# FFN weight split paced ahead of the projection, sixteen-fold heads stored by residue, last addition of the chosen and windowed heads on POOL

## The reference

```python
h = rmsnorm(x, g_mix_pre); z = h @ w_in                     # 1024 -> 33 blocks of 128 columns
o_a = nsa_mixer(...)      # 6 heads: compressed + chosen + window of 512, each times a sigmoid gate, added up
o_b = dilated_mixer(...)  # 12 heads in 3 pairs (window, fold) = (128, 1), (512, 4), (2048, 16)
o_c = banded_attention(...)  # 6 heads, window of 128, with sinks
x = x + rmsnorm(concat(o_a, o_b, o_c) @ w_out, g_mix_post)
x = x + rmsnorm(conv_glu_ffn(rmsnorm(x, g_ffn_pre), w_up, conv_w, conv_b, w_down), g_ffn_post)
```

## Time and profile before

| | us |
|---|---|
| runs (3): median, lowest, highest | 3597.2, 3593.09, 3601.05 |
| the profiled execution's own time | 3595.68 |
| its span, first to last instruction | 3593.9 |
| PE busy | 3413.3 (95%) |
| DVE, ACT, POOL busy | 1412.2, 1164.7, 512.1 |
| mean granted clock of PE | 0.978 of full speed |

### The profile page before, as it was taken

The page is one execution under the profiler, slowest core; times in us unless marked ns, Lnnn a source line. Parts: engine busy times, 40 slices in busy tenths (PEclk is TensorE's granted clock), DMA queues, the critical chain, the costliest instruction groups (busy, mean ns, idle before and its releaser), DMA issues. The chain is left out here.

```text
span 3593.9 us, 45309 instructions
## 1 busy us (share of the span) xinstructions
PE 3413.3 (95%) x16530; PEld 2720.9 (76%) x16530; DVE 1412.2 (39%) x3874; ACT 1164.7 (32%) x1980; POOL 512.1 (14%) x409
## 2 busy tenths in 40 slices
PE   8999999995898999999989969999999999999997
PEld 6788888875787876666657858887888788878886
DVE  5111101104666776666654434412541154115421
ACT  5111111114655765455433323301331133104310
POOL 1454444441000012221010000000000000000000
PEclk9999999997999999999989989999999999999999
DMA  6987765566968732332127665566556655665553
GB/s 200 324 289 258 258 224 176 203 228 178 218 166 200 170 93 59 96 94 55 51 77 234 199 218 193 193 234 233 192 196 234 228 196 197 234 216 206 196 191 117
DMA packets 297668, 676.17 MB, mean 188 GB/s; under 512 B 98704, under 2 KB 154512, under 8 KB 283408
## 3 DMA queue, kind: packets, MB, share of 16 engines
q1 hardware_dynamic: 265616, 517.93, 45.1%
q0 software_dynamic: 31840, 155.40, 12.1%
HBM read 496.06 MB, written 185.57 MB: 190 GB/s over the span
## 5 line engine op out<-in xcount | busy, mean ns | idle before, releaser
L1855 PE MATMUL f_banks<-low,f_w_hi 128*128 128x512 f32 x2816 | 871.3, 390 | 27.1 <-DMA f_w_lo<-f_lo 19.8
L1855 PEld LDWEIGHTS f_banks<-low,f_w_hi 128*128 128x128 f32 x2816 | 529.8, 188 | 140.4 <-issue 25.4
L1855 PE MATMUL f_banks<-low,f_w_lo 128*128 128x512 f32 x1408 | 548.8, 390 | 0.0
L1211 PE MATMUL a_ot_ps<-a_turned_w,a_vs 128*65 128x256 f32 (+3 forms) x1452 | 448.7, 421 | 1.1 <-issue 1.1
L493 PE MATMUL z_banks<-h_hi,z_w_hi 128*128 128x512 f32 x972 | 388.3, 399 | 7.0 <-POOL z_w_lo L305 7.0
L493 PE MATMUL z_banks<-h_lo,z_w_hi 128*128 128x512 f32 x972 | 385.3, 396 | 0.0
L493 PE MATMUL z_banks<-h_hi,z_w_lo 128*128 128x512 f32 x972 | 385.2, 396 | 0.0
L1855 PEld LDWEIGHTS f_banks<-low,f_w_lo 128*128 128x128 f32 x1408 | 265.0, 188 | 54.5
L1282 ACT ACTIVATE w_small<-w_small,a_negm 128x128 f32<-128x128 f32 (+3 forms) x510 | 249.4, 519 | 173.4 <-DVE a_negm L1361 108.3
L1875 PE MATMUL f_banks<-f_w_hi,f_g_hi 128*128 128x512 f32 x704 | 278.4, 396 | 0.0
L1875 PE MATMUL f_banks<-f_w_hi,f_g_lo 128*128 128x512 f32 x704 | 278.4, 396 | 0.0
(11 more groups left out here) (212 smaller groups left out, 5302.3 us busy)
## 6 DMA issues: line engine op xcount, KB each, us to landing
f_w_hi<-f_hi SPq DMA_DIRECT2D x264, 512.0 KB, 3.5
f_w_lo<-f_lo SPq DMA_DIRECT2D x264, 512.0 KB, 4.5
z_xs<-in_w_ffn POOLq DMA_DIRECT2D x33, 1024.0 KB, 8.6
f_hi<-z_v_hi POOLq DMA_DIRECT2D x33, 1024.0 KB, 4.9
f_lo<-z_xs POOLq DMA_DIRECT2D x33, 1024.0 KB, 6.4
low<-z_hi SPq DMA_DIRECT2D x48, 512.0 KB, 7.7
z_hi<-st_hi SPq DMA_DIRECT2D x84, 256.0 KB, 4.5
z_lo<-st_lo SPq DMA_DIRECT2D x84, 256.0 KB, 5.1
```

Source lines behind the costliest of these rows:

```text
L1211: last = pe.matmul(ot_ps[0:out_width(g), at:at + count * P], values, rows, start=(x == 0), stop=(x == len(blocks) - 1), skip_group_check=True)
L1855: last = pe.matmul(banks[:, bank, :], w[:, s % RING, c * P:(c + 1) * P], h[:, c, :], start=(c == 0 and x == 0), stop=(c == DC - 1 and x == 2))
```

## The change

Four edits. (1) POOL's loop in `project` starts at j = 1, does `split_w(j + 2)` first and then one `split_v`, two at j = 4, 8 and 12, so that the 33 pieces end at j = 30. (2) The two 4 MB copies are cut into 16 pairs of 256 KB pieces, one pair after each of the blocks 6 to 21. (3) Blocks 7, 8, 18 and 19 (queries and keys of the four heads with fold 16) are written to the staging by residue: a bank's tokens go to all four slots, so that the stores of such a block wait for all four banks, and its first bank waits for all four stores of the block before; `attend` then reads query and keys of fold 16 as 128 neighbouring elements. (4) The addition to `oh` in w and s units goes to POOL (`add_rows`), whose list in `attend` is now ordered by step together with the mixing; DVE's product into `add` waits for POOL's previous addition.

```diff
+RESIDUE_BLOCKS = (7, 8, 18, 19)
+TWICE = (4, 8, 12)
+MOVES = tuple(range(6, 22))
...
+        def by_residue(bank):
+            return bank.rearrange("p (l m a) -> p m a l", m=4, a=4)
+        def residues(tile, n):
+            return tile[:, :, 0:512].rearrange("p m (a l) -> p m a l", a=4)[:, :, :, n * P // 4:(n + 1) * P // 4]
...
-                    sp.wait_ge(w1_moved, 16)
+                    sp.wait_ge(w1_moved, 16 * len(MOVES))
...
-                    sp.wait_ge(zlo_done, lowered_through(j, n))
+                    sp.wait_ge(zlo_done, lowered_through(j, 3 if j in RESIDUE_BLOCKS else n))
...
+                    elif j in RESIDUE_BLOCKS and n == 0:
+                        for m in range(4):
+                            act.wait_ge(stored[m], stores_through(j - 1))
...
+                    if j in RESIDUE_BLOCKS:
+                        act.activation(residues(st_hi, n), by_residue(bank), ACT.Copy).then_inc(zhi_done, 1)
...
+            def move(i):
+                m, c = divmod(i, len(MOVES) // 2)
+                rows = slice(c * (CMP * HD * 2 // len(MOVES)), (c + 1) * (CMP * HD * 2 // len(MOVES)))
+                pool.dma_start(w1_copy[m, rows], w1[m, rows]).then_inc(w1_moved, 16)
+                rows = slice(i * (D // len(MOVES)), (i + 1) * (D // len(MOVES)))
+                pool.dma_start(wo_copy[rows], w_out[rows]).then_inc(wo_moved, 16)
...
-            pool.dma_start(w1_copy, w1).then_inc(w1_moved, 16)
-            pool.dma_start(wo_copy, w_out).then_inc(wo_moved, 16)
-            for j in range(NZ):
-                if j >= 1 and j + 2 < NZ:
+            v = 0
+            for j in range(1, NZ):
+                if j + 2 < NZ:
                     split_w(j + 2)
-                split_v(j)
+                for _ in range(2 if j in TWICE else 1):
+                    if v < NZ:
+                        split_v(v)
+                        v += 1
+                if j in MOVES:
+                    move(MOVES.index(j))
...
+                    if j in RESIDUE_BLOCKS and n == 0:
+                        for m in range(1, 4):
+                            dve.wait_ge(stored[m], stores_through(j - 1))
...
+                        if j in RESIDUE_BLOCKS:
+                            low, high, bank = residues(st_lo, n), residues(st_hi.bitcast(F32), n), by_residue(bank)
+                        dve.tensor_tensor(low, bank, high, ALU.subtract).then_inc(zlo_done, 1)
...
+            def add_rows(g):
...
+                if g % 4 == 0:
+                    pool.wait_ge(oh_in[s], 16 * (m // 2) + 16)
+                pool.wait_ge(added, g - late + 1)
...
+                pool.tensor_tensor(rows, rows, add[:], ALU.add).then_inc(out_done, 1)
...
+            for n in range(first_chosen * NT, N + 6):
+                if n - 2 in mix_steps:
+                    t = mix_steps.index(n - 2)
+                    mix_pairs(t)
...
+                if n - 7 in mix_steps:
+                    t = mix_steps.index(n - 7)
+                    share_out(t)
...
+                if n % 4 == 1 and (n - 9) // 4 >= late:
+                    add_rows((n - 9) // 4)
...
+                if unit.fold == NT:
+                    query = q2[:, qs, res * P:(res + 1) * P]
...
+                    if unit.fold == NT:
+                        hi, lo = (k[:, res * P:(res + 1) * P] for k in (k_hi[ks], k_lo[ks]))
...
-                if g:
+                if g > late:
+                    pe.wait_ge(added, g - late)
+                elif g:
                     pe.wait_ge(out_done, g)
...
+                    dve.wait_ge(out_done, g)
                     dve.tensor_tensor(add[:], on[:, :, 0:HD], coef[:].unsqueeze(2).to_broadcast([P, 4, HD]),
-                                      ALU.mult).then_inc(chain, 1)
-                    dve.wait_ge(chain, at + 3)
-                    dve.tensor_tensor(rows[:, :, 0:HD], rows[:, :, 0:HD], add[:], ALU.add).then_inc(out_done, 1)
+                                      ALU.mult).then_inc(added, 1)
```

More of the change, by code:

```diff
@@ L289, in _ @@
                     bank, out = banks[:, 4 * (j % 2) + n, :], st_hi[:, n, :]
-                    if is_plain(j):
+                    if j in RESIDUE_BLOCKS:
+                        act.activation(residues(st_hi, n), by_residue(bank), ACT.Copy).then_inc(zhi_done, 1)
+                    elif is_plain(j):
                         act.activation(out.bitcast(F32).rearrange("p (o u) -> p o u", o=2), by_parity(bank),
@@ L410, in _ @@
                         dve.wait_ge(zhi_done, 4 * j + n + 1)
-                        dve.tensor_tensor(st_lo[:, n, 0:512], bank, st_hi[:, n, :].bitcast(F32),
-                                          ALU.subtract).then_inc(zlo_done, 1)
+                        low, high = st_lo[:, n, 0:512], st_hi[:, n, :].bitcast(F32)
+                        if j in RESIDUE_BLOCKS:
+                            low, high, bank = residues(st_lo, n), residues(st_hi.bitcast(F32), n), by_residue(bank)
+                        dve.tensor_tensor(low, bank, high, ALU.subtract).then_inc(zlo_done, 1)
         @blk.tensor
@@ L862, in attend @@
     pick_batch = {batch["pick"]: b for b, batch in enumerate(batches) if "pick" in batch}
-    steps = {"b": 1, "c": 2, "w": 3, "s": 3, "k": 5}
+    steps = {"b": 1, "c": 2, "w": 2, "s": 2, "k": 5}
     links = [sum(steps[kind[x // 4]] - (kind[x // 4] == "k" and units[x // 4].h % R == 0) for x in range(g))
@@ L868, in attend @@
     first_chosen = kind.index("w")
+    late = 4 * first_chosen
     mix_steps = [(kind.index("w") + x) * NT + y for x in range(1, 9) for y in (4, 12)]
@@ L944, in attend @@
         out_done = sem("out_done")
+        added = sem("added")
         stored = [sem("stored0"), sem("stored1")]
@@ L1065, in _ @@
                 if u == NU - 2:
-                    sp.wait_ge(wo_moved, 16)
+                    sp.wait_ge(wo_moved, 16 * len(MOVES))
                     for c in (0, 1, 2, 3, 7):
@@ L1124, in _ @@
                 load_parts(k)
-            for t in range(NT):
-                k = t % 2
-                mix_pairs(t)
-                pool.wait_ge(tot_done, 2 * t + 2)
-                if t + 2 < NT:
-                    load_parts(t + 2)
-                share_out(t)
-                pool.wait_ge(ob_done, t + 1)
-                pool.dma_start(o_mid[t * P:(t + 1) * P, :], o_b[:, k].rearrange("p h d -> p (h d)"))\
-                    .then_inc(ob_out[k], 16)
+            def add_rows(g):
+                u, i = g // 4, 4 * (g % 4)
+                n = out_at.of_unit[u]
+                s, m = out_at.slot[n], n - out_at.of_unit[first_chosen]
+                if g % 4 == 0:
+                    pool.wait_ge(oh_in[s], 16 * (m // 2) + 16)
+                pool.wait_ge(added, g - late + 1)
+                if g > late:
+                    pool.wait_ge(out_done, g)
+                rows = oh[:, s, i:i + 4, 0:HD]
+                pool.tensor_tensor(rows, rows, add[:], ALU.add).then_inc(out_done, 1)
[3 more added lines that the diff above has]
+                    mix_pairs(t)
+                    pool.wait_ge(tot_done, 2 * t + 2)
+                    if t + 2 < NT:
+                        load_parts(t + 2)
+                if n - 7 in mix_steps:
+                    t = mix_steps.index(n - 7)
+                    share_out(t)
+                    pool.wait_ge(ob_done, t + 1)
+                    pool.dma_start(o_mid[t * P:(t + 1) * P, :], o_b[:, t % 2].rearrange("p h d -> p (h d)"))\
+                        .then_inc(ob_out[t % 2], 16)
+                if n % 4 == 1 and (n - 9) // 4 >= late:
+                    add_rows((n - 9) // 4)
             for k in range(2):
@@ L1375, in finish @@
                     rows = oh[:, s, g % 4::4, :]
-                if g % 4 == 0 and n >= 2:
+                if g % 4 == 0 and n >= 2 and g < late:
                     dve.wait_ge(stored[s], out_count[n - 2])
@@ L1410, in finish @@
                 else:
-                    if g % 4 == 0:
-                        m = n - out_at.of_unit[kind.index("w")]
-                        dve.wait_ge(oh_in[s], 16 * (m // 2) + 16)
                     column = 3 * unit.h + (2 if unit.kind == "w" else 1)
```

## The result

| | before | after |
|---|---|---|
| median of 4 runs, us | 3599.12 (3593.09 to 3601.79) | 3564.82 (3558.06 to 3565.77) |
| ratio, with its 95% interval | | 0.9903 (0.9885 to 0.9921) |
| profiled execution: time, span | 3595.68, 3593.9 | 3558.06, 3556.3 |

The medians are 34.3 us apart; 34.1 were forecast, and the time lies in the range. The profiled execution is the fastest of the four, so its own 37.6 us hold some scatter.

A forecast was written before the change was run, and what follows sets the result against it. PE was taken to bound the kernel, busy 3413 of 3594 us, so gains come from its idle time, low clock or shorter matmuls. 9.3 + 17.7 + 6 + 1.5 - 0.4 = 34.1 us; 3597.2 - 34.1 = 3563, range 3551 to 3577.

The forecast's parts named there:

- Start of project: PE's 7.0 us wait for block 4's weights at 127 us and 2.3 us of slow stretch behind it go: 9.3 us.
- End of project: POOL finishes its FFN pieces before PE, so the barrier falls at 807.6 in place of 825.4: 17.7 us.
- the second load of compress: Second 2 MB load at compress's start, needed 12 us after issue: held hidden, costing at most 5 us.
- Doubled pieces: POOL doing two FFN pieces delays the next weight split to 32.4 us, needed at 44.8; 12 us left, no cost.
- Writing by residue: Project's burst of stores and strided copies, up to twice as long, stay within the 22.4 us cover: no cost.
- Reading by residue: Contiguous operands in the four fold-16 heads of attend: 6 us gained of at most 13.9, as DMA is full.
- 2.5 + 2.5 + 1: Gains in us expected in fold-16 heads b8, b10 and b11, together 6.
- the wait of b10 for its table longer, not shorter: Sign in attend: b10, 4.91 us late for its bias table, waits longer because time saved in b9 is only waited for.
- the closing chains at b8 and the choosing of blocks at b10: DVE's work in these fold-16 heads, named in taking 2.5 us of gain for each.
- The addition: Moving w and s units' addition from DVE to POOL: 1.5 us, half the 3.1 us upper end; 0.4 us lost at attend's end.
- The rival in which it becomes a link of the chain: POOL's addition in attend holds up DVE and PE in each group: 38 us slower, 3635; chance 0.04.
- 0.62, 0.16, 0.10 and half of 0.06: Chances of forecast, larger gain, compress waiting for loads, and doubled pieces delaying weights; given as 0.92 for over 0.2% faster.

The follow-up runs named there:

- e5: Kernel before with only the two 4 MB copies cut into 16 pairs of pieces, POOL's old order kept; 3591.6 us, ratio 0.9978.
- e6: Kernel before with only POOL's new loop order, both 4 MB copies whole at the start; 3568.0 us, ratio 0.9914.
- e8: Changed kernel with one doubled FFN piece instead of three, so the pieces end two blocks later; 3577.4 us, ratio 0.9938 to the kernel before.
- e2: Kernel before with only the writing and reading by residue for fold 16; 3592.6 us, ratio 0.9990.
- e9: Kernel before with fold-16 queries read contiguously, keys still strided, using other tokens' queries; 3593.8 us in one run.
- e11: Kernel before with the next bias table loaded ahead of the next keys, for units before the first w; 3592.0 us, ratio 0.9979.
- e4: Changed kernel with the next bias table loaded ahead of the next keys, before the first w unit; 3555.4 us, ratio 0.9885 to the kernel before.

## Why the prediction was right, and which steps were not

**Start of project, 9.3 us: right in size, wider in cause than needed.** The stop and the slow stretch are gone. DVE's last subtraction ends at 794.3 to 795.7 in the seven traces with either edit of POOL's duty, mean 795.0, and at 803.7 to 805.6 in the seven without, mean 804.4: 9.4 us. I had put it to the two edits together; e5 and e6 show that each is enough.

**End of project, 17.7 us: right.** 17.9 measured, POOL as the holder shown by e8, and the second load of compress hidden as forecast (36.99 us against 37.23).

**Doubled pieces, nothing: right, with the slack near what was worked out.** POOL of the changed kernel, the weight splits around the first doubled piece:

```profile
149.84 2.38 POOL L321 TENSOR_TENSOR z_w_lo<-z_w_raw,z_w_hi 128x1024 fp32r<-128x1024 f32 x1 [10.81 <-ACT z_w_hi L264]
...
179.23 2.40 POOL L321 TENSOR_TENSOR z_w_lo<-z_w_raw,z_w_hi 128x1024 fp32r<-128x1024 f32 x1
```

They are 29.4 us apart instead of 22.4, so the second comes 7.0 us late, where 30 us against 22.4 had made it 7.6. It ends at 181.6, and PE begins that block at about 193.0 (its first bank is copied at 198.63, and takes 5.60 of PE): 11 us were left, where I had counted 12. PE never waits for `z_w_lo`.

**Writing by residue, nothing: right for PE, but both sizes were off.** ACT at the first bank of block 8, behind residue block 7, in order of time:

```profile
230.65 1.09 ACT L305 ACTIVATE st_hi<-z_banks 128x512 fp32r<-128x512 f32 x2 [13.69 <-DMA z_lo<-st_lo]
```

Groups by form from 150 to 560 us, L305 being the strided copy and L310 the plain one, L445 DVE's subtraction over both (busy time, mean ns of one, idle time before and what ended it):

```profile
L445 DVE TENSOR_TENSOR st_lo<-z_banks,st_hi 128x512 fp32r<-128x512 f32 x60 | 41.3, 691 | 294.7 <-ACT st_hi L310 216.0 <-ACT st_hi L305 78.7
L310 ACT ACTIVATE st_hi<-z_banks 128x512 fp32r<-128x512 f32 x44 | 26.3, 598 | 209.6 <-PE z_banks L526 209.6
L305 ACT ACTIVATE st_hi<-z_banks 128x512 fp32r<-128x512 f32 x16 | 9.3, 598 | 76.5 <-PE z_banks L526 53.4 <-DMA z_lo<-st_lo 23.1
```

ACT takes the first bank of block 8 at 230.65, 9.6 us after its turn (it had been idle for 13.69, and a bank's turn comes after 4 to 5), where I had forecast 4.4. The cover was wider than my 22.4 us too: the kernel gives this bank of PSUM to block 10, whose first matmul comes seven banks of 5.60 us behind the bank's turn, 39.2 us, so that 29.6 were left. And a copy out of PSUM with a stride of 16 elements costs nothing at all: 598 ns, and 598 without. I had allowed up to twice as much from the SBUF row. The statement of the Trainium skill about PSUM's lines of 8 bytes (SBUF — State Buffer, Door 1: The DMA port swizzle), read as a price on ACT and DVE too, is not borne out: it speaks of matmuls, and these copies show none.

**Reading by residue, 6 us: too much by 2.5, with a step that failed.** The profiled execution shows 6.1 us for the stretch, but that is luck: over all traces it is 3.5, so my 2.5 + 2.5 + 1 was 2.5 too much. The step that failed is that the loads are what holds the gain back, with "the wait of b10 for its table longer, not shorter" as its sign. The wait grew at k5, the unit right behind b8 and b9: 3.4 to 4.0 us in the four traces with the reading (after, e2, e8, e9), 1.0 to 1.8 in the seven without. At b10 it fell, to 1.42 us in the profiled execution and 3.0 to 3.6 in the other three, from 4.5 to 5.6. Together the two waits are as long with the reading as without (mean 6.5 and 6.4 us). They come from the place of two small tables in SP's list, and with them gone the reading gives 3.0 us. What I had no term for is DVE: as PE's matmuls get shorter, PE waits longer for DVE to have read the scores (2.8 to 6.8 us between e11 and e4), and once falls to its lower clock behind it. I had named DVE only for the closing chains at b8 and the choosing of blocks at b10.

**The addition, 1.5 us: too small by half, and its bound was no bound.** 3.3 us measured, 4.9 with no addition. I had taken PE's longest wait for DVE, 3.1 us, as the upper end, and read no other row. The wait groups of after against before (same stretch of 620 us) show the gain in several places: PE's wait for DVE's `a_turned_w` went from 3.1 to 2.3, PEld's for the same from 2.1 to 1.3, PEld's for DVE's `a_peak` from 7.8 to 6.5, and PE's for ACT's `a_turned_w` from 1.2 to 0.4. These four sum to 14.2 us before, of which 3.7 went; some overlap, so they don't add up to the gain exactly, but the bound should have been taken from all of them. POOL's addition took 0.68 us, forecast 0.61. The rival in which it becomes a link of the chain did not come: DVE never waits for POOL's `a_oh`. At the end of attend the store is issued 1.27 us after DVE's product began (1811.12 to 1812.39), where before it was 0.98 (1851.98 to 1852.96): 0.3 us lost, 0.4 forecast.

In all: 9.4 + 17.9 + 3.5 + 3.3, the last with the loss at its end in it, is 34.1 us, against the forecast's 9.3 + 17.7 + 6 + 1.5 - 0.4 = 34.1 and 34.3 between the medians. Two of the terms were right within 0.2 us; the errors of the other two, 2.5 too much and 2.2 too little (3.3 for a net 1.5 - 0.4), cancelled each other. What no edit touches, from the last store of attend to the end of the span, takes 1740.9 us before and 1743.9 after, and 1739.0 to 1745.3 in the other twelve traces, so this difference is scatter. In the chances, 0.62, 0.16, 0.10 and half of 0.06 make 0.91, and not 0.92.

## What to carry to other kernels

When an engine with slack has its work queued behind a load, ask which of two things would free it, the load coming sooner or the order changing, and try each alone: here either one sufficed, while the barrier at the end only gave way to the order. Where PE is next to a full DMA, look at what stands in the issuing engine's list ahead of the small table that is waited for last, before taking bandwidth as the limit: moving such tables ahead of the keys gave 8.5 us in its stretch, a change of data layout 3.5. And where matmuls get shorter, look at who else works in the same steps: here PE lost most of 13.9 us again, in part at least to waits for DVE. Average a stretch over all the traces that have it; one profiled execution had made a 3.5 us term look like 6.1.

## What the runs showed of the hardware that was not expected

- The beat of these 128-column float32 matmuls was set by the operand that is loaded as weights. With 64 bytes between its elements, a 128x128 weight load took 0.31 us and not 0.19, and matmuls came every 0.22 us and not every 0.11. The same stride in the streamed operand left the beat at 0.11 (e9).
- ACT and DVE read PSUM with a stride of 64 bytes at no extra cost (ACT 598 ns against 598; DVE 0.69 us for each bank of block 7 and for each plain bank of block 9), while a stride of 32 bytes in SBUF doubled ACT's copy.
- POOL adds 128x256 elements in 682 ns, where its product of the same size took 610, and DVE's addition 447.
